# Sample attention of a decoder step: values taken per key-value head on four column groups of TensorE

## The reference

```python
o_cmp, p_cmp = compressed_attention(q_plain, ctx['kc'], ctx['vc'], pos)
idx = select_blocks(p_cmp, pos, ctx['ks'].shape[2])
o_sel = selected_attention_blocked(q_rot, ctx['ks'], ctx['vs'], idx, pos, qblk)
o_win = window_attention(q_rot, ctx['wk'], ctx['wv'], pos, ctx['wpos'])
o = (gates[:, :, 0] * o_cmp.reshape(hs) + gates[:, :, 1] * o_sel.reshape(hs)
     + gates[:, :, 2] * o_win.reshape(hs))
```

## Time and profile before

| | |
|---|---|
| median of 3 runs | 1199.32 us (1199.32 to 1201.18) |
| the profiled execution's own time | 1200.1 us, span 1198.4 us |
| PE busy | 1073.2 us, 90% of the span |
| DVE, ACT, POOL busy | 826.8, 562.0, 267.5 us |
| matmuls of the values, L858 | 224 instructions (two for each float32 matmul) in 810.4 to 895.8 us of the span |

### The profile page before, as it was taken

One profiled execution on the slowest core, in us unless ns is written; L12 is line 12 of the kernel. 1 busy time (PEld: TensorE's weight loads), 2 busy tenths in 40 slices (PEclk: granted clock), 3 DMA queues, 4 the chain that ended last, 5 costly groups with the idle time before them and its releaser, 6 DMA issues.

```text
span 1198.4 us, 19330 instructions
## 1 busy us (share of the span) xinstructions
PE 1073.2 (90%) x6916; PEld 706.9 (59%) x6916; DVE 826.8 (69%) x1311; ACT 562.0 (47%) x1146; POOL 267.5 (22%) x392
## 2 busy tenths in 40 slices
PE   3789999989859999999969997789989599999995
PEld 0555566555536666666546765436666366666663
DVE  5689997999676777753483567866445777777434
ACT  2421112212456666664463336754455476666542
POOL 1385554772001121100010113004410012111000
PEclk9799998999879999999979996889999799999998
DMA  8799978665311444334602541017883133333441
GB/s 348 310 356 351 351 277 294 225 205 222 148 71 71 149 156 167 119 113 159 226 30 78 172 138 56 2 53 217 278 297 124 71 141 142 141 141 109 146 147 45
DMA packets 52531, 205.04 MB, mean 171 GB/s; under 512 B 7250, under 2 KB 36050, under 8 KB 41810
## 3 DMA queue, kind: packets, MB, share of 16 engines
q1 hardware_dynamic: 49362, 195.40, 45.0%
q0 software_dynamic: 3072, 8.39, 2.3%
HBM read 199.39 MB, written 4.38 MB: 170 GB/s over the span
## 4 chain that ended last, share of the span: by engine, by line
PE 78%; DVE 10%; ACT 4%; DMA 3%; issue 3%; SPq 2%; POOL 1%; DVEq 0%; ACTq 0%; POOLq 0%
PE PS L473 17%; PE PS L472 16%; PE PS L476 15%; PE PS L624 9%; PE PS L485 4%; DVE space L1416 4%; PE PS L858 3%; PE PS L653 2%; PE PS L496 2%; DMA x_sb<-x 2%; DVE wk_sb L1416 2%; DVE rinv L1420 1%; PE PS L606 1%; PE PS L775 1%; PE PS L811 1%
## 5 line engine op out<-in xcount | busy, mean ns | idle before, releaser
L472 PE MATMUL PS<-space_rounded 128*128 128x320 f32 x1344 | 567.3, 422 | 30.6 <-DVE space L1416 23.9
L473 PE MATMUL PS<-space_rounded,lo 128*128 128x320 bf16 x1344 | 428.3, 319 | 0.0
L476 PE MATMUL PS<-space,ring 128*128 128x320 bf16 x1344 | 403.4, 300 | 0.0
L1416 DVE TENSOR_TENSOR lo<-ring,space_rounded 128x1024 bf16<-128x1024 f32 (+1 forms) x172 | 205.8, 1200 | 218.4 <-ACT space_rounded L958 216.8
L472 PEld LDWEIGHTS PS<-space_rounded 128*128 128x128 f32 x1344 | 256.1, 191 | 98.3 <-DVE space L1416 29.1
L958 ACT ACTIVATE space_rounded<-ring 128x1024 fp32r<-128x1024 f32 (+1 forms) x172 | 176.9, 1033 | 224.8 <-PE PS L473 224.8
L473 PEld LDWEIGHTS PS<-space_rounded,lo 128*128 128x128 bf16 x1344 | 129.8, 97 | 125.8 <-issue 4.3
L476 PEld LDWEIGHTS PS<-space,ring 128*128 128x128 bf16 x1344 | 135.7, 101 | 0.0
L624 PE MATMUL PS<-space 128*128 128x256 f32 x512 | 115.2, 383 | 0.0
L624 PEld LDWEIGHTS PS<-space 128*128 128x128 f32 x512 | 96.3, 191 | 28.9 <-issue 16.4
L485 PE MATMUL PS<-ring,silc 128*32 128x512 f32 x448 | 68.3, 687 | 32.2 <-DMA ring<-w_mod 16.6
(11 more groups left out here) (213 smaller groups left out, 1369.8 us busy)
## 6 DMA issues: line engine op xcount, KB each, us to landing
ring<-w_mod SPq DMA_DIRECT2D x24, 2048.0 KB, 9.6
ring<-w_up SPq DMA_DIRECT2D x22, 2048.0 KB, 8.1
ring<-w_down SPq DMA_DIRECT2D x16, 1408.0 KB, 5.9
space<-pool_cmp SPq DMA_DIRECT2D x128, 128.0 KB, 2.8
ring<-w_mod_kv SPq DMA_DIRECT2D x4, 2048.0 KB, 10.4
ring<-w_kv SPq DMA_DIRECT2D x3, 2048.0 KB, 8.4
ring<-w_glu SPq DMA_DIRECT2D x2, 2048.0 KB, 10.6
ring<-w_q SPq DMA_DIRECT2D x2, 2048.0 KB, 8.1
```

What stands on the lines that cost most here:

```text
L472: pe.matmul(out, wr[:, p % SPLIT, at:at + P], xr[:, k, :], start=start, stop=False)
L473: mm = pe.matmul(out, lo[:, p % SPLIT, at:at + P], xh[:, k, :], start=False, stop=False)
L476: return pe.matmul(out, w, xl[:, k, :], start=False, stop=stop)
L1416: return dve.tensor_tensor(out, a, b, op)
```

## The change

For each of the 14 products one matmul of 128 stationary by 256 moving columns becomes four, one for each head, of 32 stationary by 64 moving columns, each into its own 32 partitions of bank 7, columns 0 to 63. The wanted blocks then lie in the same 64 columns of all partitions, and ACT copies them with one instruction, twice side by side, into OD (the second copy takes the place of the zeros; the scatter behind the transpose reads only the wanted half). The count on semaphore `od` is adapted.

```diff
                 for c in range(4 * n, min(4 * n + 4, len(ops))):
-                    mm = pe.matmul(PS[:, 7, 0:256], ops[c][0], ops[c][1], start=(c == 0), stop=(c == len(ops) - 1))
+                    for hd in range(KVH):
+                        mm = pe.matmul(PS[32 * hd:32 * hd + 32, 7, 0:HD], ops[c][0][:, 32 * hd:32 * hd + 32], ops[c][1][:, HD * hd:HD * hd + HD],
+                                       start=(c == 0), stop=(c == len(ops) - 1))
...
-                pe.wait_ge(S("od"), KVH * (j - NPJ + 1))
+                pe.wait_ge(S("od"), j - NPJ + 1)
...
-                for hd in range(KVH):
-                    act.activation(OD[32 * hd:32 * hd + 32, HD * (hd % 2):HD * (hd % 2) + HD],
-                                   PS[32 * hd:32 * hd + 32, 7, HD * hd:HD * hd + HD], ACT.Copy).then_inc(S("od"), 1)
+                act.activation(OD.rearrange("p (e f) -> p e f", e=2), PS[:, 7, 0:HD].unsqueeze(1).broadcast_to([P, 2, HD]),
+                               ACT.Copy).then_inc(S("od"), 1)
```

## The result

The changed kernel takes 1194.3 us (median of 20 runs, 1190.0 to 1198.0), the kernel before 1199.3 us in the same series (20 runs, 1196.1 to 1201.9). The ratio is 0.9957, 95% interval 0.9946 to 0.9969: faster by 5.2 us, 3.7 to 6.5. The forecast was 1193 with 0.77 for faster.

What follows compares the result with a forecast made beforehand. TensorE bound the sample rounds (11.46 us), the SP queue close behind (11.08 us a pass). The projection starting 8.0 us earlier, less 1.3 us for the clock, saves 6.7 us: 1193 us, range 1189.5 to 1198.5.

Steps and rivals of the forecast that it cites:

- rival B: Sample rounds: clock falls in most, scores at half clock, k loop 11.5 us a round; 1195.5 to 1199 us; chance 0.15.
- the sum: Whole kernel: projection starts 8.0 us earlier, less 1.3 us for the clock, gives 6.7 us saved.
- The price of the values: Values on TensorE: 112 instructions at 30 ns, 3.3 us a round in place of 6.4, saving 3.1 us.
- Rival C: Sample values: instructions limit small matmuls, near 57 to 62 ns; round stays 11 to 11.5 us; 1196 to 1202; chance 0.12.
- rival D: Sample values: weight load and matmul pair costs over 65 ns, with stalls at tile switches; at 86 ns, 1226 us; chance 0.07.
- The shortest round: Sample round, scores to `pv_mm`: the unchanged softmax chain on ACT allows no less than about 9.05 us.
- The queue: SP queue in the sample rounds: sets the pace from the second round on, 11.08 us a pass without pause.
- the new bound: Sample stage: SP queue takes over from TensorE as what limits the rounds; 1190 to 1195.5 us; chance 0.60.
- rival E: Sample rounds: SP queue passes get shorter too, 10.77 us everywhere, and the clock holds; 1187 to 1190 us; chance 0.06.
- The end: Last round to projection: o0 issued after v7 at 875.6, landing at 885.2, first projection matmul at 890.8, 8.0 us earlier.
- The clock: TensorE's clock in scores and projection start: idle gaps slow it, costing 1.3 us, between 0 and 5.
- ACT: ACT's copies into OD: four become one, 0.7 us less a round, hidden and worth nothing while cover holds.

Runs made afterwards that it cites:

- e8: Changed kernel with each matmul of the values issued twice into the same sum; 1205.6 us, 1.0051 of the kernel before.
- e2: Changed kernel with window parts of k3 to k7 and v1 to v7 issued by ACT's queue instead of SP's; 1194.2 us, ratio 0.9956.
- e7: Changed kernel with half window parts, issued by ACT's queue, and idle-time matmuls in the rounds; 1192.8 us, ratio 0.9943.
- e3: Changed kernel with window parts issued by ACT's queue and idle-time matmuls in the rounds; 1194.7 us, ratio 0.9943.
- e6: Changed kernel with half window parts, these issued by ACT's queue; 1193.3 us, ratio 0.9945.
- fillers: Idle-time matmuls with unused output added to the changed kernel, in the rounds (1193.7 us, 0.9944) or around the end (1193.4 us, 0.9957).
- e12: Changed kernel, but ACT copies the four blocks with four instructions as before; 1195.0 us, ratio 0.9962.
- e5: Changed kernel loading only half of each window part for k3 to k7 and v1 to v7; 1193.5 us, ratio 0.9952.
- e1: Changed kernel plus 25 idle-time float32 matmuls ahead of values and scores in the rounds; 1193.7 us, ratio 0.9944.

## Why the forecast came out right, point by point

The time is 1194.3 where 1193 was said, and faster. Part of that is luck. The clock fell in five of the seven rounds, which was the condition of rival B (chance 0.15), not of the forecast, and the five rounds from the second scores to the last took 11.4 us each in the profile, nearer to B's 11.5 than to the forecast's 11.1. The profiled execution, 1196.6, lies in B's range; the median lies in the forecast's. The two profiled executions differ by 3.5 us where the sum says 6.7, the medians by 5.0. By its own steps:

*The price of the values.* I took 30 ns an instruction, 3.3 us a round. Measured are 32 in 0.65 us with the last one's drain, 18 ns from start to start (a group and the next transposes are 0.59 us apart), 2.3 us in the round from 835.50. The row it was read from ran at half clock, so the pace does follow the clock: in the change's last round, at half clock, 32 take 1.08 us. That was the right row with too cautious a value, and it changed nothing, since the softmax chain was already the longer. Rival C (57 to 62 ns) is refuted. The Trainium skill's 62 ns per MATMUL with hardware decoding off ("TensorE: Matmul & The Clock Gate", section "Wait — 56ns, not 53.3ns?") does not bind here, at 18 ns; no run tells how the decoding is set. Twice as many instructions (e8) do make the kernel slower than before, though by stalls and not, as in rival D, by the price of one.

*The shortest round.* 9.05 us forecast from ACT's rows; 9.06 measured from 814.54 to 823.60. Half of what the stage won lies in the first round, from scores to scores 8.8 us in place of 11.5; the next five won 0.5 us together, and from the last scores to the first L472 it was 2.0 us.

*The queue.* 11.08 us a pass forecast, 11.09 measured, without a pause. That it is "the new bound" was too simple. When it alone is relieved (e2), rounds are hardly shorter (11.3 us): the pages' landings take longer (medians 4.0 and 4.2 us for 3.4 and 3.8), and scores run at half clock in three rounds of seven. With all three relieved (queue, bytes, clock; e7) they are 10.5 us. I read this as three bounds within a microsecond of each other, of which one taken away uncovers the next; the time doesn't show it, since e3, e6 and e7 gave the gain back at the end. Mis-sized were the landings: the forecast took 5.0 us for win_k and 4.6 for win_v from the medians of before, and where TensorE waited they took 6.0 (k4), 6.4 (k6) and 6.67 (v2). The pass of 10.77 us that rival E names isn't in the rows, which give 10.83.

*The end.* I had v7's issue follow the fifth pass at once, and o0 issued at 875.6. In fact v7 waited for `pv_mm` of job 5 until 871.6 and its window part took 1.94 us to issue, so that o0 was issued at 878.30; its landing took 9.27 us (9.6 in the earlier trace rows). The first L472 came at 893.1, not 890.8: 5.7 us earlier than before, not 8.0, and 0.45 of the 5.7 are a stage that began earlier (805.77 for 806.22). This is the term that was off most.

*The clock.* 1.3 us was taken, between 0 and 5. The profiles show slow scores in 5 of 7 rounds and 6.0 us of half clock in the projection against 3.4 before. Over the whole tail it is 27.0 us of half clock against 22.3, and 4.7 us more at half the pace are 2.3 us, which is what the tail is longer by. So in the profiled execution the clock took about 2.3 us behind the stage, and part of the delay of `pv_mm` of job 5 inside it. 8.0 - 2.3 (end) - 2.3 (tail) = 3.4, which is the 3.5 us that the profiles differ by. The median over 20 runs differs by 5.0; how large the clock's part is in it the runs can't tell, since fillers, which held the clock, moved no median beyond its interval. The forecast read the half clock of 800 to 804 as one with little but transposes; the timeline has as many matmuls in it (L825, 801.55, 1.12 us) as transposes (L811, 802.61, 1.12 us). What the Trainium skill says of transposes, that they don't count as activity for the clock ("TensorE: Matmul & The Clock Gate", "Part 4: PE-mode transpose"), no run here shows: the nine transposes at 882.09 in the change's last round ran at half clock, but the clock had fallen 0.1 us ahead of them, and the same nine of before (886.59) ran at full clock.

*ACT.* Forecast at nothing, measured at nothing (e12).

## What to carry to other kernels

When two bounds lie within a few per cent, price a saving by the second one: here 4 us a round less for TensorE gave 5.3 us over all eight rounds, half of it in the first, whose data had landed, because the queue's pass of 11.09 us stood right behind, with the DMA engines and the clock near it. When you move an issue to another queue, look at what it now stands behind: v7's last part behind o0 cost e3, e6 and e7 what they had won. A tile that computes only what is wanted can leave an engine idle enough to lose its clock, so compare it with a wider tile that wastes some work (two groups of 64 did as well with half the instructions). And count instructions, not only columns: between 112 and 224 matmul instructions of the values a round lay the step from faster to slower, most of it in stalls.

## What was not expected of the hardware

- On four column groups, matmul instructions of 32 stationary by 64 moving float32 columns start 18 ns apart, over 32 in a row.
- TensorE stalled eight times, up to 3.2 us, in the middle of runs of identical matmuls without any wait in the program (e8, 448 matmul and weight-load instructions of the values a round). Each ended 1.3 to 1.5 us after a 16 KB packet of the instruction queue. The change (224) had none in its profile, but e2, e5, e6 and e12, with as many instructions, had one or two each, of 0.4 to 1.0 us.
- With TensorE busy 8.7 of 11.9 us of a round the clock still fell to half, and so in each round from 823.60 on; with five float32 matmuls of about 0.5 us more in its gaps (e1) it fell once in the rounds (833.5 to 837.3) and once ahead of the projection.
- o0's 2 MB took 9.3 (the change) to 11.7 us (e1, e2) to land. A window part of 0.5 MB issued 0.53 us behind o0 took 11.3 us (e3), where before such parts took 4.6 in the median.
